# Context's norm for the convolution summed in the last down projection, its row turned in a bank of its own, clears on GpSimd, and three weight slabs at the start

## The reference, cut to what matters

```python
x = x + gt2 * ((jax.nn.silu(a) * v_ff) @ w_down[l])
```

```python
hx = rmsnorm(x, norm_g[i, 0]) * (1.0 + sc_x) + sh_x
hc = rmsnorm(ctx, norm_g[i, 0]) * (1.0 + sc_c) + sh_c
...
u = h @ w_pw1 + b_pw1
a, gt = jnp.split(u, 2, axis=-1)
u = a * jax.nn.sigmoid(gt)
u = lax.conv_general_dilated(u, w_dw[:, None, :], ..., padding=[(CONV_PAD, CONV_PAD)], ...) + b_dw
```

## Time and profile before

| what | us |
|---|---|
| device time, median of 3 runs | 3287.12 |
| span of the profiled execution (first to last instruction) | 3282.0 |
| median less span | 5.1 |
| PE busy in the span | 3152.4 |
| DVE, ACT, POOL busy | 1570.4, 1186.3, 815.1 |
| last down product to the first product of the convolution module | 1634.6 to 1657.7 on the span's clock |
| write of the first U, first taps matmul, first matmul of the third pair of jobs | 1679.75, 1693.10, 1698.88 |

### The profile page before, as it was taken

How to read it: one execution, slowest core, us unless ns; L and a number is a source line. 1 busy time by engine, 2 the same in 40 slices (tenths; PEclk the granted TensorE clock), 3 DMA queues, 4 the chain that set the end, 5 groups by cost and what they waited for, 6 DMA issues and landing times.

```text
span 3282.0 us, 38620 instructions
## 1 busy us (share of the span) xinstructions
PE 3152.4 (96%) x15546; PEld 2472.2 (75%) x15546; DVE 1570.4 (48%) x2204; ACT 1186.3 (36%) x1764; POOL 815.1 (25%) x399
## 2 busy tenths in 40 slices
PE   6999999999999999999989899999999979999998
PEld 4657778887665777778867477888888658878887
DVE  3572146464375124334378644322334899653234
ACT  3443244243444224424321244111112558632223
POOL 4302445555320343444401000000000039500000
PEclk9999999999999999999999999999999999999999
DMA  6413436665430555453335211222221110122332
GB/s 237 129 42 110 147 91 200 217 192 164 128 113 7 180 175 171 144 178 93 98 81 130 53 49 55 65 65 65 61 62 58 39 39 1 39 70 88 106 89 79
DMA packets 429892, 337.21 MB, mean 103 GB/s; under 512 B 16637, under 2 KB 411223, under 8 KB 417428
## 3 DMA queue, kind: packets, MB, share of 16 engines
q1 hardware_dynamic: 428272, 334.23, 33.5%
q0 software_dynamic: 1248, 0.46, 0.1%
q10 hardware_dynamic: 196, 0.07, 0.0%
HBM read 319.58 MB, written 2.10 MB: 98 GB/s over the span
## 4 chain that ended last, share of the span: by engine, by line
PE 58%; DVE 5%; POOL 4%; ACT 1%; issue 1%; SPq 0%; DMA 0%; POOLq 0%; DVEq 0%; ACTq 0%
PE PS L435 17%; PE PS L436 17%; PE PS L437 17%; POOL p L2579 4%; PE PS L524 1%; PE PS L831 1%; PE PS L592 1%; PE PS L637 1%; DVE both_tmp L1371 0%; DVE q_parts L1693 0%; PE PS L1026 0%; DVE Wl L1274 0%; PE PS L536 0%; DVE stat_t L1347 0%; SPq L2621 0%
## 5 line engine op out<-in xcount | busy, mean ns | idle before, releaser
L435 PE MATMUL PS<-Hh,Wh 128*128 128x512 f32 x2208 | 875.4, 396 | 20.5 <-DVE both_tmp L1371 8.3
L2534 POOL TENSOR_TENSOR Wl<-raw,Wh 128x1024 fp32r<-128x1024 f32 (+2 forms) x254 | 618.0, 2441 | 986.6 <-ACT Wh L2045 986.6
L436 PE MATMUL PS<-Hl,Wh 128*128 128x512 f32 x2208 | 861.8, 390 | 0.0
L437 PE MATMUL PS<-Hh,Wl 128*128 128x512 f32 x2208 | 861.4, 390 | 0.0
L2045 ACT ACTIVATE Wh<-raw 128x1024 fp32r<-128x1024 f32 (+2 forms) x442 | 436.1, 988 | 400.4 <-PE PS L437 349.5
L435 PEld LDWEIGHTS PS<-Hh,Wh 128*128 128x128 f32 x2208 | 416.1, 188 | 127.9 <-issue 62.6
L437 PEld LDWEIGHTS PS<-Hh,Wl 128*128 128x128 f32 x2208 | 415.8, 188 | 88.0
L436 PEld LDWEIGHTS PS<-Hl,Wh 128*128 128x128 f32 x2208 | 416.4, 189 | 67.6 <-issue 3.4
L1274 DVE TENSOR_TENSOR Wl<-raw,Wh 128x1024 fp32r<-128x1024 f32 (+3 forms) x188 | 217.6, 1157 | 389.6 <-ACT Wh L2045 389.3
L1952 DVE SCALAR_TENSOR_TENSOR cv<-PS,vcols,cv 128x510 f32<-128x510 f32 (+1 forms) x176 | 123.7, 744 | 216.8 <-ACT cv L2456 216.8
L435 PE MATMUL PS<-g_h,Wh 128*128 128x512 f32 x528 | 206.7, 391 | 3.5 <-POOL Wl L2534 3.5
(11 more groups left out here) (383 smaller groups left out, 4759.3 us busy)
## 6 DMA issues: line engine op xcount, KB each, us to landing
raw<-in_ffn_w SPq DMA_DIRECT2D x108, 512.0 KB, 3.6
mod_w<-in_w_mod SPq DMA_DIRECT2D x48, 1024.0 KB, 5.0
raw<-in_w_up SPq DMA_DIRECT2D x88, 512.0 KB, 4.6
mod_w<-in_w_ada SPq DMA_DIRECT2D x40, 1024.0 KB, 4.9
raw<-in_w_in SPq DMA_DIRECT2D x62, 512.0 KB, 4.0
UQ<-U SPq DMA_DIRECT2D x128, 99.4 KB, 2.2
raw<-in_w_down SPq DMA_DIRECT2D x32, 384.0 KB, 5.0
raw<-in_conv_w_pw SPq DMA_DIRECT2D x24, 512.0 KB, 4.1
```

Source lines behind the costliest of these rows:

```text
L435: pe.matmul(o, wh, xh, start=start, stop=False, skip_group_check=True)
L436: pe.matmul(o, wh, xl, start=False, stop=False, skip_group_check=True)
L437: return pe.matmul(o, wl, xh, start=False, stop=stop, skip_group_check=True)
L2534: pool.tensor_tensor(low, src, high.bitcast(F32), ALU.subtract).then_inc(*mark("w_low_pool", one[0]))
```

## The change

1. ("n", 0, "c") joins SUMMED. In the last half of the last down projection (l = 1) ACT also squares the context's chunk j, DVE also adds it, and PE's `down` closes both sums with one-column matmuls. The full-width statistics of the context (`pre(("n", 0, "c"), CTX)`) go.
2. `token_rows` turns both rows, x's into bank 6 and the context's into bank 7, not into work banks; a copy of the context reads its row from PSUM as x's does.
3. DVE does both `rstd`, then x's h, then splits the slabs up to the third, then the context's h. ACT does both roots, then x's high parts and the context's, with no squares between.
4. The two clears of U move from DVE to POOL, ahead of the tap weights.
5. The convolution module begins with three jobs (`linear_trio_both`): x's products of the first two jobs chunk by chunk, then x's of the third, then the context's of the first, second and third job. The third job is ("pw1a", "x", 1), so that for j = 1 only ("pw1g", "x", 1) is left.

```diff
@@ -389,7 +389,7 @@
     block_cm = nc.Block()
     block = block_cm.__enter__()
     NS = {"x": SEQ, "c": CTX}
-    SUMMED = ([("n2", l) for l in range(DEPTH)] + [("n1", 1), ("n", 0, "x"), ("post", ("att", "x")), ("post", ("ffn", 1, "x"))]
+    SUMMED = ([("n2", l) for l in range(DEPTH)] + [("n1", 1), ("n", 0, "x"), ("n", 0, "c"), ("post", ("att", "x")), ("post", ("ffn", 1, "x"))]
               + [("post", (*y, x)) for y in (("conv",), ("ffn", 0)) for x in "xc"])
     BY_TOKEN = [t for t in SUMMED if t != ("post", ("ffn", 1, "x"))]
 
@@ -494,6 +494,39 @@
                             mm.then_inc(*fill(job))
                             release[job] = full(job)
 
+        def linear_trio_both(tag, *three_jobs):
+
+            c_tag = (*tag[:-1], "c")
+            hc = h_of(c_tag)
+            tally.h_before[tag] = tally.h_before[c_tag] = tally.h_reader[0]
+            ws = []
+
+            def take(job, src, kind):
+                begin(job, "pair")
+                ws.append((job, slab(job, k_p(src), KD, src.shape[1], kind)))
+
+            def products(job, w, i, s):
+                return both(job, w, i, slice(0, P), (Hh[:, i, :], Hl[:, i, :]), (hc[0][:, i, :], hc[1][:, i, :]),
+                            i == 0, i == KD - 1, s)
+
+            take(*three_jobs[0])
+            take(*three_jobs[1])
+            for i in range(KD):
+                pe.wait_ge(*ready("h_low", tag, i))
+                for job, w in ws:
+                    products(job, w, i, "x")
+            take(*three_jobs[2])
+            for i in range(KD):
+                products(*ws[2], i, "x")
+            for n, (job, w) in enumerate(ws):
+                for i in range(KD):
+                    if n == 0:
+                        pe.wait_ge(*ready("h_low", c_tag, i))
+                    mm = products(job, w, i, "c")
+                mm.then_inc(*fill(job))
+                release[job] = full(job)
+            tally.h_reader[0] = ws[2][0]
+
         def linear_pair(tag, n, *two):
 
             tally.h_before[tag] = tally.h_reader[0]
@@ -537,12 +570,12 @@
                                start=first and t == 0, stop=final, skip_group_check=True)
             return mm
 
-        def token_rows(*tags, fill_in=(1, 2)):
+        def token_rows(*tags, fill_in=(1, 2), own_banks=False):
 
             keep_warm(fill_in[0])
             for tag in tags:
                 job, s = ("r", tag), stream(("ss", tag))
-                begin(job)
+                begin(job, ("stat" if s == "x" else "mod") if own_banks else "work")
                 pe.wait_ge(*ready("stat_r", tag))
                 for t in range(NS[s] // P):
                     mm = pe.transpose(bank(job)[:, t * P:(t + 1) * P], TOKENS[s][3][:, t:t + 1].broadcast_to([P, P]),
@@ -760,6 +793,9 @@
             token_rows(*(("post", ("ffn", 0, s)) for s in "xc"), fill_in=(1, 4))
 
         def down(name, w_src, half, n, stat_tag, after=None):
+            stat_tags = [stat_tag] if stat_tag != ("n", 0, "x") else [stat_tag, ("n", 0, "c")]
+            if half == 1 and len(stat_tags) > 1:
+                assert not queue, queue
             for j in range(KD):
                 job = (*name, half, j)
                 begin(job)
@@ -777,21 +813,25 @@
                 release[key] = full(job)
                 mods()
                 if half == 1 and j > 0 and stat_tag:
-                    norm_stat(stat_tag, j - 1, n)
+                    for t in stat_tags:
+                        norm_stat(t, j - 1, NS[stream(("ss", t))])
                 if half == 1 and after:
                     after(j)
             if half == 1 and stat_tag:
-                norm_stat(stat_tag, KD - 1, n)
-                token_rows(stat_tag)
+                for t in stat_tags:
+                    norm_stat(t, KD - 1, NS[stream(("ss", t))])
+                token_rows(*stat_tags, own_banks=len(stat_tags) > 1)
 
         def conv_both():
 
             for j in range(KD):
                 w = {x: a["conv_w_pw1_2"][0, :, c0 + j * P:c0 + (j + 1) * P] for x, c0 in (("a", 0), ("g", D))}
                 if j == 0:
-                    linear_pair_both(("n", 0, "x"), *((("pw1" + x, "x", j), w[x], "split") for x in "ag"))
+                    third = a["conv_w_pw1_2"][0, :, P:2 * P]
+                    linear_trio_both(("n", 0, "x"), *((("pw1" + x, "x", j), w[x], "split") for x in "ag"),
+                                     (("pw1a", "x", 1), third, "split"))
                 else:
-                    for x in "ag":
+                    for x in "ag"[j == 1:]:
                         linear_both(("pw1" + x, "x", j), w[x], ("n", 0, "c"))
                     quad_taps(j - 1)
             for c in range(KD):
@@ -1210,7 +1250,6 @@
                 start_mods((2, 0, 0), (2, 0, 1), (2, 0, 2), (2, 1, 0))
 
         assert not queue, queue
-        pre(("n", 0, "c"), CTX)
         conv_both()
         for s in ("x", "c"):
             pre(("f", 0, s), NS[s])
@@ -1370,11 +1409,12 @@
 
             return dve.scalar_tensor_tensor(o, x, g, STATS[s][3][rows, 0:n] if r is None else r, ALU.mult, ALU.mult)
 
-        def norm_to_h(tag, n, g, sh, gains=None, ring="one"):
+        def norm_to_h(tag, n, g, sh, gains=None, ring="one", rooted=False):
 
             s = stream(("ss", tag))
             high, lo = h_of(tag)
-            rstd(("ss", tag), n, D)
+            if not rooted:
+                rstd(("ss", tag), n, D)
             if gains:
                 gains()
             slot, by_token = {}, tag in BY_TOKEN
@@ -1461,11 +1501,14 @@
 
         def conv_both():
 
-            dve.wait_ge(*full(("dn", 1, DEPTH - 1, "x", 1, KD - 1)))
-            own(dve.memset(U[0][:, :], 0.0))
-            pads = own(dve.memset(U[1][:, :], 0.0))
-            norms_to_h("n", 0)
-            dve.wait_ge(*pads)
+            for s in ("x", "c"):
+                rstd(("ss", ("n", 0, s)), NS[s], D)
+            for s in ("x", "c"):
+                norm_to_h(("n", 0, s), NS[s], lambda c: col(2, 0, s, 6, c), lambda c: col(2, 0, s, 0, c), ring="both",
+                          rooted=True)
+                if s == "x":
+                    ahead(first_slab(("n", 0, "x")))
+            dve.wait_ge(*ready("pads", 1))
 
             def gate(j):
                 a_, g_, u, b = ("pw1a", "x", j), ("pw1g", "x", j), U[j % 2], vec("b_pw1", j)
@@ -1969,6 +2012,8 @@
                     ahead((*job, 1))
                     if half == 1:
                         sum_squares(("n1", 1) if l == 0 else ("n", 0, "x"), j - 1)
+                        if l == 1:
+                            sum_squares(("n", 0, "c"), j - 1)
                     add_to_x(job, col(1, l, "x", 5, j), j)
                 dve.wait_ge(*free(job))
                 if l == 1 and half == 0:
@@ -2110,6 +2155,9 @@
                 act.wait_ge(*full(tally.h_before[tag]))
             if between:
                 between()
+            norm_highs(tag, n, sh)
+
+        def norm_highs(tag, n, sh):
             for c in range(KD):
                 act.wait_ge(*(free(("r", tag)) if tag in BY_TOKEN and c == KD - 1 else ready("h_pre", tag, c)))
                 act.activation(h_of(tag)[0][:, c, 0:n], tb(("h", tag, c))[:, 0:n], ACT.Identity, bias=sh(c))\
@@ -2129,7 +2177,14 @@
 
         def conv_both():
 
-            norms_to_h("n", 0, lambda c: free(("x_t", "c", c)))
+            x, c = ("n", 0, "x"), ("n", 0, "c")
+            root(("ss", x), SEQ)
+            root(("ss", c), CTX)
+            ahead(first_slab(x))
+            if tally.h_before.get(x):
+                act.wait_ge(*full(tally.h_before[x]))
+            norm_highs(x, SEQ, lambda j: col(2, 0, "x", 0, j))
+            norm_highs(c, CTX, lambda j: col(2, 0, "c", 0, j))
 
             for j in range(KD):
                 ahead(("pw1a", "x", j))
@@ -2471,6 +2526,9 @@
                             ahead(first_slab(("n1", l + 1) if l + 1 < DEPTH else ("n", 0, "x")))
                         act.wait_ge(*free(job))
                         square((("n1", l + 1) if l + 1 < DEPTH else ("n", 0, "x"), j), X[:, j, :], SEQ)
+                        if l == 1:
+                            act.wait_ge(*free(("x_t", "c", j)))
+                            square((("n", 0, "c"), j), XS["c"][:, j, 0:CTX], CTX)
                 if l == 1 and half == 0:
                     load_x("c")
 
@@ -2543,6 +2601,8 @@
                 one.then_inc(*mark("tap_cols", g, i))
                 pool.wait_ge(*ready("tap_cols", g, i))
         pool.wait_ge(*full(("dn", 1, DEPTH - 1, "x", 1, KD - 1)))
+        for i in range(2):
+            pool.memset(U[i][:, :], 0.0).then_inc(*mark("pads", i))
         for j in range(KD):
             if j >= 2:
                 pool.wait_ge(*full(("taps", j - 2)))
@@ -2665,7 +2725,7 @@
 BLOCK_1_SLABS = set("kv kr ql q ukv uq k v gm gs bm bs wo up".split())
 
 SIGNALS = """const_in vec_in vec_in_rest mod_w_in mod_w_used mod_sum c_in pos_in x_in turn_in c_act angle sines
```

(2 more changed lines are left out.)

## The result

The changed kernel took 3269.78 us, median of four executions (3269.53 to 3274.40), beside 3287.97 for the kernel before: ratio 0.9948 (95% interval 0.9934 to 0.9962). The forecast was 3277.0 with a range from 3273.0 to 3280.2, so the change brought more than the range allows. In two later sets of five executions its medians were 3274.83 and 3274.94, with ratios 0.9958 (0.9946 to 0.9970) and 0.9957 (0.9944 to 0.9970).

The account below looks back on a forecast made before the run. PE was taken to bound the kernel. The third pair of jobs starting 10.1 us earlier gave a span of 3282.0 - 10.1 = 3271.9; with the median 5.1 above the span, 3277.0 us, range 3273.0 to 3280.2.

Parts of the forecast that it names:

- rival (e): Last down projection: the context's sums hold up the splits, making the kernel slower, 3288 us or more, up to 3295; chance 0.03.
- pace of the products: Convolution module's start: an x product takes 0.229 us on PE, a context product 0.118.
- wait for the copies: Before taps(0): SP's copies, no longer covered, take 11.9 us and PE stands still for 3.6 us.
- taps at the low clock: Taps(0) after PE's gap: 6.94 us instead of 5.37, a loss of 1.6 us.
- the marker: Start of the third pair of jobs in the convolution module, forecast at 1688.8 us against 1698.88, 10.1 us earlier.
- Part 2: From the last down product to the convolution module's first product, forecast at 1644.1 us (1643.5 to 1645.3).
- Part 3: The three starting jobs, then table load, sigmoid and U at once: U(0) at 1668.7 us, 11.05 us earlier.
- Rival (a): Kinder clock: rise at 1641.7, no fall before taps(0); 11.7 us gained, 3275.4 us, with luck 3273.5; chance 0.22.
- Part 5: Clears of U moved from DVE to POOL: 1.4 us per clear, no gain and no cost by itself.
- the 0.5 us that the rule was given: DVE's Newton steps beside POOL's weights: possible hold-up by SBUF contention, making the time 3277.5 rather than 3277.0 us.

Follow-up runs that it names:

- own bank alone: Kernel before with one edit: x's turned row goes to bank 6 instead of a work bank; median 3276.86 us, ratio 0.9978.
- the experiment above: Changed kernel with two jobs instead of three at the start of the convolution module; median 3269.59 us, ratio 0.9942.
- the experiment with the weights there instead: Changed kernel with the two clears of U back on DVE, so POOL makes the tap weights at once; median 3273.91 us, ratio 0.9965.

## Why the prediction was wrong

**What held.** The bound was named rightly. PE's wait was for the bank that held the turned row: own bank alone removes it (first product 23.24 to 15.79), and work banks bring it back (16.06). DVE waited on ACT behind the context's squares, and that wait is gone. The sums in the down projection hold nothing up, against rival (e): POOL's splits of the large slabs stand 7.48 us apart,

```profile
1610.05 1.83 POOL L2592 TENSOR_TENSOR Wl<-raw,Wh 128x768 fp32r<-128x768 f32 x1 [3.50 <-ACT Wh L2090]
...
1617.53 1.83 POOL L2592 TENSOR_TENSOR Wl<-raw,Wh 128x768 fp32r<-128x768 f32 x1 [3.50 <-ACT Wh L2090]
...
1625.01 1.83 POOL L2592 TENSOR_TENSOR Wl<-raw,Wh 128x768 fp32r<-128x768 f32 x1 [3.50 <-ACT Wh L2090]
```

and the 33 products of a down job (eleven chunks) at 0.227 us, the step of PE's rows there, are 7.48 us too: PE alone sets the pace. The pace of the products was right (16.44 us from the first product to the first context product, 16.5 forecast), and so were the wait for the copies as the new bound (13.18 us from U(0) to the taps against 13.1; the wait itself 3.13 against 3.6), the taps at the low clock (7.06 against 6.94), and that taps, not DVE, free the marker.

**Two terms of the sum were mis-sized, by 2.3 us together.** That alone would not have taken the result out of the range (3287.1 - 12.35 = 3274.8 lies in it); what did is that executions differ by more than the range allowed, as shown under "The range lacked a term".

Part 2, up to the first product: 8.62 against 9.67 us. The one-column sums took 3.70 us where 3.97 were forecast, the context's part 0.89 of them (1640.04 to 1640.93) for 1.0. The first keep-warm pair took 1.26 us to the transposes, not 1.75, since the clock fell 0.3 us later than forecast and found most of its first matmul done. The six transposes took 1.28 us for 1.64: x's four and the context's two run on with no pause, and the long duration of the earlier trace rows was that of a row on its own. The last four matmuls took 2.39 for 2.3. The sum is 0.27 + 0.49 + 0.36 - 0.09 = 1.03 us.

Part 3, the step "table load, sigmoid and U follow at once": 2.5 us were added behind the second job, 2.3 of them from the table load's start on. The table load does not need the bank, and ACT's split ahead of it was done: the load ran from 1666.46, ahead of the sigmoid's wait for the job, and in all five profiles with three jobs the sigmoid waits 0.41 us for PE with the load behind it. In the earlier trace rows it seemed to follow that wait because ACT's split just ahead of it ended late. From the first context product to U(0) it is 6.86 us and not 8.1: 1.24 us. The load took 1.28 us in the earlier trace rows and here; only its place moved. With two jobs the split is late again and the load with it: in the experiment above it stands at 1668.93, right behind the split, and the sigmoid starts as it ends.

Rival (a), a kinder clock, came true in one half. The clock rose 7.73 us after zero, where (a) had 7.3 and the forecast 8.5; but it fell again in the gap before the taps, as the forecast had it. Its 11.7 us are near the measured 12.35 for other reasons.

**A step that was not weighed.** The forecast priced the third job's wait for copies (3.6 us) and its taps at the low clock (1.6), and took them as part of the change, but did not ask what two jobs with the other edits would give. The decomposition, in us at the marker against the kernel before:

| own bank | sums and clears | jobs at the start | marker earlier by |
|---|---|---|---|
| yes | no | 2 | 7.8 |
| no | yes | 2 | 6.8 |
| yes | yes | 2 | 15.9 |
| no | yes | 3 | 2.4 |
| yes | yes | 3 (the change) | 12.35 |

"Sums and clears" takes in the new order of DVE's and ACT's work. Bank and sums are worth 14.6 one by one and 15.9 together, so they nearly add up. The third job takes back 3.6 with own banks and 4.4 without.

**The range lacked a term.** With both terms right, the sum would have been 3274.8, as the two later medians. The first one is 5 us lower, and that is luck of the draw. 72 executions of the kernel before, on at least two chips, lie between 3282.4 and 3293.5, mean 3287.1 with a standard error of 0.4; 14 of the changed one between 3269.5 and 3277.2, mean 3272.8 with 0.8. The three runs shown beforehand covered 2.2 us and gave the range no such spread. From the 14, an execution's standard deviation is 2.8 us, and that of a median of four about 1.7 (an estimate): the range needed some 3 us more on either side.

Where the spread comes from is partly visible. In code that is the same in both kernels the granted clock differs from one profile to the next:

```profile
430.00:460.00 30.00, 27.80 (x126) 21.74 (x126) 9.48 (x17) 11.01 (x15) 12.24 (x6) 1.00 0.36 105
990.00:1030.00 40.00, 35.80 (x147) 21.60 (x146) 26.96 (x65) 17.74 (x33) 0.00 (x0) 1.00 0.00 0
```

```profile
430.00:460.00 30.00, 28.66 (x126) 22.29 (x125) 9.30 (x17) 11.01 (x15) 12.26 (x6) 0.95 0.36 105
990.00:1030.00 40.00, 35.80 (x142) 21.71 (x141) 25.73 (x61) 16.42 (x29) 0.00 (x0) 0.96 0.00 0
```

The first two rows are the kernel before, the others the changed one. The time at the low clock ahead of zero adds up to 13.7 us in the first profile of the kernel before, 20.5 in its second, and 27.3, 34.1 and 17.1 us in the three of the changed kernel. Over all 13 profiles it goes with the position of zero (correlation 0.92, 0.33 us of delay for each us at the low clock). This is a correlation; no run set the clock's stretches, and why they differ is not shown. The changed kernel's mean gain is 3287.1 - 3272.8 = 14.3 us, standard error 0.9, where the stretch gives 12.35. The other 2.0 is some two standard errors, has no place in the profiles (1583.3, 1583.4 and 1581.7 us behind the marker, before 1583.1 and 1583.0), and stays open.

**The clears and the steps that POOL holds up.** Part 5 had a clear on POOL at 1.4 us; it took 0.75. The steps of `der` with both inputs in SBUF, while the clears ran (1637.52 to 1639.01), took 0.24 us for two; in the experiment with the weights there instead, the same pairs took 0.51 and 1.13. In the changed kernel one Newton step with both inputs in SBUF (L1386, 1640.82) took 0.41 beside the weights (to 1641.20) against 0.16 elsewhere, and the one ahead of it that reads PSUM was not held. By the rule of the Trainium skill, "SBUF — State Buffer", section "Who interferes with whom", that the forecast had weighed, this is what should happen: the trace agrees, for clears too. The price, 0.25 us, was covered by the first keep-warm pair, so the 0.5 us that the rule was given did not arise. The cover was thinner than forecast: x's numbers were ready at 1641.62 and its row was turned at 1642.19, 0.57 us to spare where 1.6 were counted.

## What to carry to other kernels

When a change puts several cures together, ask of each what the rest would give without it: here the bank gave 7.8 us, the sums 6.8, both 15.9, and the third cure, longer work at the start, took 3.6 back, since the work it pulled ahead of U had been the cover of U's copies. Time a step from what the instruction itself waits for, not from the row ahead of it: a table load that stands behind a split in the old trace may run long before the data is there. Before a range is drawn from three runs, ask how far executions of one kernel lie apart, and measure small changes by positions from a common event, after looking how well these repeat (here 0.1 us for the marker, 0.3 for points where the clock changes).

## What the runs showed of the hardware that was not expected

ACT's table load does not wait for the operands of the activation behind it: it ran from 1666.46 to 1667.74, the activation waited until 1668.15, and so in all five profiles with three jobs. POOL clears 128 x 813 fp32 elements in 0.75 us, at DVE's pace (0.74), though its two-input work on 512 columns takes 1.05. And the code ahead of the change, the same instructions in the same order but for the sums, took up to 9 us more or less from one profile to the next (zero at 1633.45 to 1642.61), along with 13.7 to 37.5 us at the low clock. The code behind the marker took 1578.8 to 1583.4 us in the same 13 profiles.
